# Gated state space: issuing the decay products of a bank's two heads in turn for each key tile

## The chip, the cores and the metric

The kernel runs on one core of a Trainium2 chip. The metric is the time that the device takes for one execution, in microseconds (us). TensorE does the matrix products and writes them to PSUM; VectorE (DVE), ScalarE (ACT) and GpSimd (POOL) work beside it, and the queue of SyncE (SP) issues most of the transfers. Engines wait for each other through semaphores.

## What is computed

The reference is two blocks of two layers each over 512 tokens of width 1024. The change lies in one part of it, the gated state space mixer (Mamba-2) in the second layer of the first block:

```python
xs, Bm, Cm = jnp.split(xbc, [SSM_D_INNER, SSM_D_INNER + G * N], axis=-1)
dt = jax.nn.softplus(dt + dt_bias);  A = -jnp.exp(A_log)
a = (dt * A).reshape(b, nc, CHUNK, G, R)
...
seg = jnp.exp(jnp.where(tril, a_cs[..., :, None] - a_cs[..., None, :], -jnp.inf))
cb = jnp.einsum('bclgn,bcsgn->bcgls', Cm, Bm)
y_diag = jnp.einsum('bcgls,bcgrls,bcsgrp->bclgrp', cb, seg, x_dt)
...
y = y_diag + y_off + xs * D_skip
g = y * jax.nn.silu(z);  g = g * lax.rsqrt(jnp.mean(g * g) + EPS)   # per group
return g @ w_out
```

There are 8 groups of 4 heads, and a head has 64 channels. The kernel computes the same sum without the chunks of 64: for each head one lower triangular matrix over all 512 tokens, decay times C·B, multiplied with x·dt.

## The kernel before

The stage is a loop over 8 groups (group 0, six in a hardware loop of two at a time, group 7). In each group TensorE runs, in this order: `pe_ssm_scores` (turns the two x tiles and makes C·B), `pe_ssm_norm` of the group before, one 256-column unit of the next group's input projection, `pe_ssm_heads(c, 0)`, a second unit, `pe_ssm_heads(c, 1)`, a third unit. A unit is 48 matmuls of 512 columns at lines 529 to 531 (three for each product, with the operands split in a high and a low part). In group 7 the units are the first ones of the output projection.

`pe_ssm_heads(c, m)` works on heads 2m and 2m+1 of the group. Both write one PSUM bank: the even head partitions 0 to 63, the odd head partitions 64 to 127 (`a = (hd % 2) * HD`). For one head there are 4 matmuls, one per key tile i, since a key tile of 128 tokens acts only on the queries from its own start on: 512, 384, 256 and 128 columns. The stationary operand is `XDT`, 128 rows by 64 columns, so that it uses half of the array's columns. `DECAY[:, hd % 2]` is the moving operand. The data is fp32, and the trace shows two passes (a weight load and a matmul each) for one such instruction. So one call is 8 instructions and 16 passes, and there are 16 calls.

What feeds it: VectorE writes the differences of the running sums into `DECAY` (`dve_ssm_decay`, line 2343), ScalarE takes the exponential (line 2305), VectorE multiplies by the masked C·B (`dve_ssm_mask`, line 2351), and counts `masked` up once per head. `DECAY` has two buffers, one for an even and one for an odd head. Before VectorE overwrites the even one for head 2, it waits for `first_head`, which TensorE counts up at the last matmul of head 0. Before it overwrites the odd one for head 3, it waits until the bank of heads 0 and 1 is complete (`bank_ready`). `dve_ssm_output` reads both banks.

The order of VectorE in a group: scores, decay of heads 0 and 1, mask of heads 0 and 1, root of the group before, convolution 0 of the next group (line 2245), decay of 2 and 3, mask of 2 and 3, convolution 1, output. GpSimd splits the weights of the coming units (lines 832 to 837), each as soon as the unit two before it is done, and SP loads the raw weights when GpSimd has split the ones before.

Of the kernel before, what the change touches and what calls it, by code (L numbers as in the profile page):

```python
# [24 lines left out]
NT = SEQ // P  # L25
# [5 lines left out]
HD = 64  # L31
# [202 lines left out]
def build(nc, t, out):  # L234
# [3 lines left out]
    def sem(name):  # L238
        return ctx.enter_context(nc.semaphore(name))
# [252 lines left out]
    bank_ready = sem("bank_ready")  # L492
# [17 lines left out]
    def take_bank(pe, b, turns=0):  # L510

        if b // 4 + (0 if isinstance(turns, int) else 1) > 0:
            pe.e.wait_ge(bank_free[b % 4], turns + b // 4)
        return BANK[b % 4]
# [1690 lines left out]
    def turns(e, n):  # L2205

        return 0 if e is None else e * n
# [49 lines left out]
    def ssm_heads_bank(c, m):  # L2257
        return plan.b["ssm"] + 8 * c + 5 + m
# [20 lines left out]
    def pe_ssm_heads(pe, e, c, m):  # L2279

        w = ssm_sems
        bank = take_bank(pe, ssm_heads_bank(c, m), turns(e, 4))
        for hd in (2 * m, 2 * m + 1):
            a = (hd % 2) * HD
            pe.wait(w["masked"])
            for i in range(NT):
                ins = nc.tensor.matmul(bank[a:a + HD, i * P:SEQ], XDT[:, i, hd * HD:hd * HD + HD],  # L2287
                                       DECAY[:, hd % 2, TRI_AT[i]:TRI_AT[i] + SEQ - i * P], start=i == 0, stop=i == NT - 1)
            if hd == 0:
                ins.then_inc(w["first_head"], 1)  # L2290
            elif hd % 2:
                ins.then_inc(bank_ready, 1)

    def pe_ssm_norm(pe, e, c):
        pe.wait(sq_ready)
# [96 lines left out]
    def pe_ssm(pe):  # L2392
        w = ssm_sems

        def unit(e, c, j):
            if c < SSM_G:
                pe_ssm_unit(pe, e, c, j)
            else:
                pe_ssm_out_unit(pe, 0, j)

        def group(e, c):
            pe_ssm_scores(pe, e, c)
            if c:
                pe_ssm_norm(pe, e, c - 1)
            unit(e, c + 1, 0)
            pe_ssm_heads(pe, e, c, 0)
            unit(e, c + 1, 1)
            pe_ssm_heads(pe, e, c, 1)
            unit(e, c + 1, 2)

        first_unit(pe, plan.u["ssm"], take_pair(pe, plan.p["ssm"]), pe.seen(h_ready))
        pe.passed(h_ready, KD)
        pe_logits(pe, plan.b["dt"], DT_WH, DT_WL, SSM_H, False)
        unit(None, 0, 1)
        pe_dt_rows(pe)
        unit(None, 0, 2)
        pe_dt_columns(pe)
        ssm_program(pe, group, {w["conv_ready"]: 4, w["masked"]: 8, sq_ready: 2})
        pe_ssm_norm(pe, None, SSM_G - 1)
        pe_ssm_out_unit(pe, 0, 3)  # L2420
# [1396 lines left out]
```

## Time and profile before

| | |
|---|---|
| median of 3 runs | 2789.88 us (2789.29 to 2791.4) |
| span of the profiled execution | 2789.68 us |
| TensorE matmul busy | 2515.7 us, 90% of the span |
| VectorE busy | 1800.4 us, 65% |
| GpSimd busy | 1468.6 us, 53% |
| ScalarE busy | 964.0 us, 35% |
| state space stage, from about 680 to 1040 us | 360 us |

The span is the time from the first to the last instruction of one profiled execution. The profile gives no other time for that execution; its span is 0.2 us below the median of the runs. Matmuls are pipelined, and a matmul's record is longer than the distance to the next, so starts are what is to be read, not the sum of durations. "PE" is the matmul and "PEld" the weight load.

### The profile page before, as it was taken

The page shows a single profiled execution, that of the slowest core. Times are in us where ns is not written, and L with a number is a line of the kernel's source. Part 1 is how long each engine was busy: PE and PEld are TensorE (multiplying, and loading weights), DVE is VectorE, ACT ScalarE, POOL GpSimd, SP SyncE. Part 2 cuts the span into 40 slices and gives each one's busy share as a digit, 9 for nine tenths or more (in the row PEclk, how much of TensorE's full clock was granted, in tenths as well). Part 3 has the DMA queues.
Part 4 walks back from the last instruction along what each step waited for, and adds up shares of the span by engine and source line. Part 5 has one row for each costly group of instructions (what it writes and reads, how often), then busy time and mean ns, then how long its engine had stood idle before and what let it go on. Part 6 is the DMA issues. An engine that isn't in the chain of part 4 may idle for free.

```text
span 2789.7 us, 36720 instructions
## 1 busy us (share of the span) xinstructions
PE 2515.7 (90%) x12718; PEld 1994.1 (71%) x12718; DVE 1800.4 (65%) x2200; ACT 964.0 (35%) x1494; POOL 1468.6 (53%) x1234
## 2 busy tenths in 40 slices
PE   4968989968999999899687889999996789999998
PEld 2754767856777778678476558888885678888887
DVE  6669866757676766667678766666136954666324
ACT  2013257733444432577422323222014632222102
POOL 4730333436454443344355216676778937666775
PEclk8977989989999999899888789999998999999999
DMA  8735579952323322699532113333232123333222
GB/s 314 253 128 206 187 252 328 320 177 77 98 83 98 96 77 98 239 335 320 183 80 80 64 53 93 103 90 102 91 109 61 39 54 94 103 91 105 87 94 83
DMA packets 319122, 386.73 MB, mean 139 GB/s; under 512 B 51578, under 2 KB 259214, under 8 KB 318902
## 3 DMA queue, kind: packets, MB, share of 16 engines
q1 hardware_dynamic: 261424, 335.84, 36.8%
q10 hardware_dynamic: 34438, 28.08, 3.3%
q0 software_dynamic: 23168, 21.59, 2.3%
q8 instruction: 57, 0.93, 0.1%
q14 instruction: 35, 0.29, 0.0%
HBM read 397.62 MB, written 55.41 MB: 162 GB/s over the span
## 4 chain that ended last, share of the span: by engine, by line
PE 36%; POOL 19%; issue 17%; DVE 14%; DMA 10%; ACT 2%; SPq 0%; ACTq 0%; POOLq 0%; DVEq 0%
POOL WL L837 14%; PE PAIR L529 6%; PE PAIR L530 5%; PE PAIR L531 5%; POOL WH L833 5%; PE PAIR L1842 4%; DMA RAW<-in_ffn_w_up 3%; PE BANK L529 2%; PE BANK L530 2%; PE BANK L531 2%; PE BANK L2287 2%; DMA RAW<-in_moe_w 2%; PE PAIR L1812 2%; DMA ADA_A<-in_ada_w 2%; DVE ADA_SUM L634 1%
## 5 line engine op out<-in xcount | busy, mean ns | idle before, releaser
L837 POOL TENSOR_TENSOR WL<-RAW,WH 128x512 fp32r<-128x512 f32 x584 | 817.6, 1430 | 12.2
L529 PE MATMUL PAIR<-HH,WH 128*128 128x512 f32 x1792 | 710.6, 397 | 57.2 <-POOL HL L1126 30.8
L530 PE MATMUL PAIR<-HL,WH 128*128 128x512 f32 x1792 | 701.0, 391 | 0.0
L531 PE MATMUL PAIR<-HH,WL 128*128 128x512 f32 x1792 | 700.5, 391 | 0.0
L832 POOL TENSOR_TENSOR TURN<-ONES 128x1 f32<-128x1 f32 x146 | 34.7, 238 | 914.3 <-PE PAIR L531 837.3
L529 PEld LDWEIGHTS PAIR<-HH,WH 128*128 128x128 f32 x1792 | 338.5, 189 | 141.8 <-issue 44.6
L531 PEld LDWEIGHTS PAIR<-HH,WL 128*128 128x128 f32 x1792 | 338.4, 189 | 71.4
L530 PEld LDWEIGHTS PAIR<-HL,WH 128*128 128x128 f32 x1792 | 338.8, 189 | 70.9 <-issue 2.4
L833 POOL TENSOR_SCALAR WH<-RAW 128x2048 fp32r<-128x2048 f32 x146 | 281.0, 1925 | 0.0
L2022 POOL DMA_INDIRECT XG<-htok_scratch,GATHER_I x78 | 106.0, 1359 | 259.0 <-PE PAIR L1812 153.0
L529 PE MATMUL BANK<-WH,GH 128*128 128x256 f32 x624 | 181.0, 290 | 0.0
L530 PE MATMUL BANK<-WL,GH 128*128 128x256 f32 x624 | 173.9, 279 | 0.0
L531 PE MATMUL BANK<-WH,GL 128*128 128x256 f32 x624 | 173.8, 278 | 0.0
L1842 PE MATMUL PAIR<-W2RAW,HT 128*128 128x512 f32 x312 | 147.9, 596 | 6.8 <-ACT HT L1884 5.3
L529 PE MATMUL PAIR<-FHH,WH 128*128 128x512 f32 x352 | 138.7, 394 | 0.0
L531 PE MATMUL PAIR<-FHH,WL 128*128 128x512 f32 x352 | 138.0, 392 | 0.0
L530 PE MATMUL PAIR<-FHL,WH 128*128 128x512 f32 x352 | 136.6, 388 | 0.0
L1949 DVE TENSOR_TENSOR WL<-RAW,WH 128x1024 fp32r<-128x1024 f32 x78 | 95.6, 1226 | 57.1 <-ACT WH L1760 57.1
L1943 DVE TENSOR_TENSOR GL<-PAIR,GH 128x1024 fp32r<-128x1024 f32 x78 | 95.5, 1224 | 52.5 <-ACT GH L1878 52.5
L1812 PEld LDWEIGHTS PAIR<-IDENT,XG 128*128 128x128 f32 x624 | 83.3, 192 | 60.9 <-issue 34.4
L2832 DVE TENSOR_TENSOR X<-PAIR,X 128x1024 f32<-128x1024 f32 x8 | 9.8, 1225 | 179.3 <-PE PAIR L531 179.3
L2794 DVE TENSOR_TENSOR PAIR<-PAIR,RSTD 128x1024 f32<-128x1024 f32 x44 | 54.2, 1232 | 110.0 <-PE PAIR L531 109.9
(530 smaller groups left out, 4878.2 us busy)
## 6 DMA issues: line engine op xcount, KB each, us to landing
RAW<-in_moe_w SPq DMA_DIRECT2D x156, 512.0 KB, 6.9
RAW<-in_ffn_w_up SPq DMA_DIRECT2D x88, 512.0 KB
W2RAW<-in_moe_w SPq DMA_DIRECT2D x78, 512.0 KB, 6.1
ADA_B<-in_ada_w SPq DMA_DIRECT2D x30, 1024.0 KB, 5.4
RAW<-in_ssm_w_in SPq DMA_DIRECT2D x48, 512.0 KB
ADA_A<-in_ada_w SPq DMA_DIRECT2D x18, 1024.0 KB, 7.3
RAW<-in_ffn_w_down SPq DMA_DIRECT2D x32, 512.0 KB
RAW<-in_ev_w_in SPq DMA_DIRECT2D x20, 512.0 KB
```

What stands on the lines that cost most here:

```text
L529: nc.tensor.matmul(o, wh, xh, start=start, stop=False)
L530: nc.tensor.matmul(o, wh, xl, start=False, stop=False)
L531: return nc.tensor.matmul(o, wl, xh, start=False, stop=stop)
L833: pool.tensor_scalar(WH[:, s], RAW[:, s], 1.0, 1.0, ALU.mult, ALU.mult).then_inc(split_hi, 1)
L837: ins = pool.tensor_tensor(WL[:, s, c], RAW[:, s, c], WH[:, s, c].bitcast(F32), ALU.subtract)
L1812: ins = nc.tensor.transpose(pair[:, k // 4, (k % 4) * P:(k % 4) * P + P], rows_of(s)[:, :, k], IDENT[:])
L1842: ins = nc.tensor.matmul(pair[:, m, :], HT[:, s % 2, :], W2RAW[:, s % 2, c], start=True, stop=True)
L1943: dve.e.tensor_tensor(GL[:, s % 2].rearrange("p (b k) n -> p b (k n)", b=2), PAIR[p % 2][:], GH[:, s % 2].rearrange("p (b k) n -> p b (k n ...
L1949: dve.e.tensor_tensor(WL[:, u % 2, 0:D], RAW[:, u % 2, 0:D], WH[:, u % 2, 0:D].bitcast(F32), ALU.subtract).then_inc(w["w1_low"], 1)
L2022: pool.e.indirect_dma_start(XG[:, s % 2, :], None, htok_dram, bass.IndirectOffsetOnAxis(ap=GATHER_I[:, s:s + 1], axis=0), bounds_check=SEQ ...
L2287: ins = nc.tensor.matmul(bank[a:a + HD, i * P:SEQ], XDT[:, i, hd * HD:hd * HD + HD], DECAY[:, hd % 2, TRI_AT[i]:TRI_AT[i] + SEQ - i * P], ...
L2794: dve.e.tensor_tensor(pair[:], pair[:], bcast(RSTD[:], 1, 2), ALU.mult).then_inc(w["scaled"], 1)
```

## The change

The two heads of a bank were issued one after the other, each behind its own wait for `masked`. Now one wait for both stands ahead, and for each key tile the even head's matmul is followed by the odd head's. The operands, the places in PSUM, the number of matmuls and their start and stop flags stay. `first_head` is counted up at head 0's last matmul as before, which is now the last but one of the call; `bank_ready` at the last matmul of the call.

```diff
-        for hd in (2 * m, 2 * m + 1):
-            a = (hd % 2) * HD
-            pe.wait(w["masked"])
-            for i in range(NT):
+        pe.wait(w["masked"], 2)
+
+        for i in range(NT):
+            for hd in (2 * m, 2 * m + 1):
+                a = (hd % 2) * HD
                 ins = nc.tensor.matmul(bank[a:a + HD, i * P:SEQ], XDT[:, i, hd * HD:hd * HD + HD],
                                        DECAY[:, hd % 2, TRI_AT[i]:TRI_AT[i] + SEQ - i * P], start=i == 0, stop=i == NT - 1)
-            if hd == 0:
-                ins.then_inc(w["first_head"], 1)
-            elif hd % 2:
-                ins.then_inc(bank_ready, 1)
+                if hd == 0 and i == NT - 1:
+                    ins.then_inc(w["first_head"], 1)
+        ins.then_inc(bank_ready, 1)
```

## Rows read from the trace of the kernel before

**Rows 1.** Busy time by stretch; columns: PE, PEld, DVE, ACT, POOL, clock, DMA

```profile
680.00:1040.00 360.00, 359.30 (x1545) 263.32 (x1544) 266.10 (x354) 146.07 (x141) 171.46 (x142) 1.00 0.30 92
1040.00:1110.00 70.00, 70.00 (x322) 56.34 (x320) 39.49 (x67) 20.94 (x32) 31.22 (x30) 0.98 0.24 83
```

**Rows 2.** Who waited for whom, 680 to 1040 us: total, times, longest

```profile
POOL TURN L832 <- PE PAIR L531: 182.0, 23, 9.1
ACT CONV L2224 <- PE PAIR L531: 53.2, 14, 4.4
...
DVE XDT L2321 <- PE BANK L2269: 45.1, 7, 7.2
...
PE PAIR L529 <- DVE HL L2525: 0.7, 1, 0.7
```

**Rows 3.** Groups of instructions by shape, TensorE, 680 to 1040 us

```profile
L2287 PE MATMUL BANK<-DECAY,XDT 128*64 128x512 f32 x64 | 34.3, 618 | 0.0
```

**Rows 4.** Chain of work that ended last, 737.1 to 741.2 us: start, us, what

```profile
737.25 2.30 PE BANK L2287 x8
739.55 0.10 issue
739.65 1.46 PE BANK L2287 x6
741.11 0.43 PE PAIR L529
```

**Rows 5.** The same chain, 680 to 1040 us: turns, then C·B

```profile
767.18 0.87 PE BANK L2269 x8
768.05 2.16 PE BANK L2275 x8
```

**Rows 6.** Timeline of the weight loads of one bank, from 751.2 us

```profile
752.14 0.19 PEld L2287 LDWEIGHTS BANK<-DECAY,XDT 128*64 128x64 f32 x2 [0.35 <-issue]
752.63 0.14 PEld L2287 LDWEIGHTS BANK<-DECAY,XDT 128*64 128x64 f32 x1 [0.29 <-issue]
...
753.70 0.62 PEld L2287 LDWEIGHTS BANK<-DECAY,XDT 128*64 128x64 f32 x6 [0.18 <-issue]
754.62 0.14 PEld L2287 LDWEIGHTS BANK<-DECAY,XDT 128*64 128x64 f32 x1 [0.29 <-issue]
```

**Rows 7.** Timeline of TensorE: 32-column tiles in turn, and full-width turns

```profile
2146.37 2.02 PE L3313 MATMUL BANK<-HF,IDENT 128*32 128x128 f32 x32 [1.11 <-DVE HF L1149]
...
767.02 1.03 PE L2269 MATMUL BANK<-IDENT,CONV 128*128 128x128 f32 x8
```

**Rows 8.** Timeline around the second bank of a group: TensorE, then VectorE

```profile
752.14 3.93 PE L2287 MATMUL BANK<-DECAY,XDT 128*64 128x512 f32 x16
756.00 0.50 PE L529 MATMUL PAIR<-HH,WH 128*128 128x512 f32 x1
...
733.98 3.34 DVE L2372 RECIPROCAL RSTD<-RSTD 128x512 f32<-128x512 f32 x1
...
743.61 3.13 DVE L2343 TENSOR_SCALAR DECAY<-ACS_ROW,ACS_COL 128x512 f32<-128x512 f32 x8
747.41 2.89 DVE L2351 TENSOR_TENSOR DECAY<-DECAY,CBM 128x1280 f32<-128x1280 f32 x2 [0.67 <-ACT DECAY L2305]
```

**Rows 9.** Timeline of group 7 and of a first bank: TensorE, then VectorE

```profile
1012.11 3.93 PE L2287 MATMUL BANK<-DECAY,XDT 128*64 128x512 f32 x16
...
1009.58 2.88 DVE L2351 TENSOR_TENSOR DECAY<-DECAY,CBM 128x1280 f32<-128x1280 f32 x2
...
816.38 5.41 DVE L2343 TENSOR_SCALAR DECAY<-ACS_ROW,ACS_COL 128x512 f32<-128x512 f32 x8
```

**Rows 10.** Chain of work, 998 to 1005 us: TensorE released by VectorE

```profile
998.74 1.56 DVE HL L2525
1000.30 0.14 issue
```

**Rows 11.** Waits of SP's queue, 1040 us to the end

```profile
SPq L683 <- POOL WL L837: 1027.2, 98, 42.3
```

## Prediction

> **What bounds the kernel now.** I read the busy time by stretch first. From 680 to 1040 us, which holds the whole state space stage, TensorE is busy 359.3 of 360 us at a granted clock of 1.00 of full speed, that is at the upper level of 2.4 GHz; VectorE has 266 us, ScalarE 146, GpSimd 171 [rows 1]. Then the waits of that stretch: the long ones all belong to other engines that wait for TensorE (GpSimd 182.0 us, ScalarE 53.2, VectorE 45.1), while TensorE's one wait of note is 0.7 us, for the split input of group 7 [rows 2]. So the stage ends when TensorE's instructions are through, and time taken out of TensorE's stream comes out of the span one to one, until another engine is late.
>
> Next, how long a bank of decay products takes. Its matmuls are 128 rows by 64 columns of stationary operand; the records of the widest last 618 ns each, though their starts are closer together [rows 3], so I go by starts and by the chain. The timeline has one at 752.14 and the next unit's first matmul at 756.00: 3.86 us [rows 8]. All 16 banks have this length (the same record of 3.93 us stands at 752.14 and at 1012.11 [rows 8, 9]). Their 16 passes are not simply added up: the chain shows head 0's eight passes as 2.30 us, then 0.10 us of issue, then only six passes in 1.46 us, and the next unit [rows 4]. Head 1 also has eight passes, so its first two, the widest, lie beside head 0's. The weight loads show where: in the bank at 752.14, two loads come together, then one by one, each as its matmul starts; at 753.70 six stand back to back, and then single ones again at 754.62 [rows 6]. A load row lists passes in order of time, so the six are head 0's last three and head 1's first three. **At the crossing from head 0 to head 1 the array works on both heads at once**, one in the lower and one in the upper half of its columns. If they ran one after the other, the bank would take 2.30 us plus the cost of the same columns without an overlap: C·B has eight passes of the same widths (512, 384, 256, 128, two each) and takes 2.16 us in the chain [rows 5], so 2.30 + 2.16 = 4.46 us. The bank of today already saves 0.60 us against that, by the one crossing.
>
> Why only one crossing: head 1's first pass gets in when head 0's fifth starts and the load of its sixth is issued, the first of the six. So only what stands behind a few pending instructions of head 0 gets in. In the order of today the second head's instructions lie behind all four of the first head's; in the new order each is next to its partner.
>
> **The change part by part.**
>
> The order. With the heads in turn both halves of the array have work from the start to the end of the bank. Head 0's eight passes last as long as alone (2.30 us by the chain), and head 1's run beside them. What goes is the issue gap and head 1's tail: 0.10 + 1.46 = 1.56 us [rows 4]. Head 1 begins a moment after head 0; I take 0.02 us for this, an estimate, since loads issued back to back in the six-load row leave room for little more (0.62 us for six loads of about 0.14 us each, which overlap in part) [rows 6]. Gain of a bank: 1.54 us. 16 banks: 24.6 us.
>
> Do two halves keep full speed when both are busy throughout? The trace has the nearest case in another stage: at 2146.37 four tiles of 32 columns are issued in turn, 32 passes of 128 columns, in 2.02 us; eight full-width passes of 128 columns, one after the other, take 1.03 us [rows 7] and 0.87 us net in the chain [rows 5], 0.109 us each. One after the other the 32 would take 24 x 0.109 + 1.03 = 3.65 us. So issuing in turn does let the tiles run together, and four of them give 3.65 / 2.02 = 1.8 times the speed, or about two tiles' worth. Two tiles should then reach nearly two. Bounds: the best end is 1.56 us a bank (25.0 in all). The other end takes that ratio of 2.02 / 3.65 = 0.55 as it stands, with all its start and end in it, though 32 short passes suffer more from these than a bank does: 4.46 x 0.55 = 2.47 us instead of 2.30, a gain of 3.86 - 2.47 = 1.39 us, 22.2 us in all. I take the value near the best end, as the crossing of rows 4 is the same instruction, tile and data type, and there head 0's passes keep their length.
>
> The wait. `masked` for both heads now stands ahead of head 0. Nothing is queued behind it on TensorE that could go ahead of it; the unit before it is already issued. It costs nothing where both masks are there when TensorE arrives. First banks: the bank at 737.25 [rows 4] has VectorE begin the reciprocal that stands behind both its masks at 733.98 [rows 8], some 3 us early, and nothing before that bank becomes faster within the group. Second banks: the masks end at 747.41 + 2.89 = 750.30 and TensorE arrives at 752.14, 1.84 us later [rows 8]. Now TensorE arrives 1.54 us sooner, as counted from the end of the unit that starts this chain (ScalarE's read, VectorE's convolution, decay, exponential, mask). 0.30 us is left, and a hand-over from VectorE to TensorE takes up to 0.14 us where the chain shows one [rows 10]. So the cover just holds: 0. It is thin; each 0.1 us by which the chain slips behind costs 0.7 us over the seven second banks that have this layout. Group 7, first bank: TensorE arrives at 1012.11 and the second mask ends at 1009.58 + 2.88 = 1012.46 [rows 9]. Head 0 could start with the first mask alone; now it waits 0.35 us and the hand-over: 0.4 us lost, once. That group's second bank has masks of VectorE's own pace and more room after this delay; I take 0.
>
> The signals. `first_head` comes with head 0's last pass, as before some 2.3 us after the bank's start; it is now also slightly behind head 1's sixth. `bank_ready` comes 1.54 us sooner. VectorE meets neither late: head 2's decay starts at 743.61, more than 4 us after both [rows 8]. Nothing else moves: no DMA, no instruction of another engine and no queue is passed; TensorE issues one wait less.
>
> What is late next: GpSimd and the transfers follow TensorE. GpSimd waited 182 us in 23 places for a unit, about 8 us each [rows 2], and will wait up to 1.5 us less. After the stage TensorE is busy 70.0 of 70 us [rows 1], and later SP's loads wait for GpSimd's splits, 98 times [rows 11], so that all that follows moves forward as one piece. I keep the whole gain.
>
> **The sum**: 24.6 - 0.4 = 24.2 us. The profiled span is 2789.7 us and the median of the runs 2789.9, so both lose the same, and the forecast is 2789.9 - 24.2 = 2765.7 us.
>
> **The rivals.**
>
> Partly together. Two halves share something that slows each, and the gain of a bank is below 1.39 us. For it: four tiles reach only 1.8 times. Against it: this is what a limit of two streams would give, and two halves are two streams. Its time: 22.2 - 0.4 gives 2768.1 at the bound above; with half of the gain, 12.3 - 0.4, 2778.0. The Trainium skill, "TensorE: Matmul & The Clock Gate", section "Measured speedup vs the span model", has three column tiles at 2.38 times, 0.79 of the ideal; by that (an estimate) two would give 1.59 times, and the sum would come to about 2773.
>
> The thin cover fails. The eight decay instructions take 3.13 us ahead of a second bank [rows 8], but 5.41 us at another place, where GpSimd works beside them [rows 9]. Were they 2.3 us longer at seven second banks, TensorE would wait 2.3 - 0.16 = 2.1 us in each, 15 us: 2780.7. Against it: GpSimd's split and this chain both start from the same unit's end, so they lie to each other as before.
>
> Slower: the halves don't overlap when issued in turn, and the one overlap of today is lost too. It would be so if a load for the other half had to wait for the matmul that runs, and the crossing were a case of its own, say because head 0 had nothing more to load. Then each bank takes 4.46 us, 0.60 more; 16 x 0.60 + 0.4 = 10.0 us, 2799.9. It decides as soon as a bank takes over 3.86 us. Against it stands the row with four tiles in turn, which is 1.8 times faster than one after the other [rows 7]. The Trainium skill, same page, section "The mechanism", states that weight loads overlap matmuls in flight only where the row group differs, and that matmuls start and end strictly in order; both heads use all 128 rows, so by that rule this rival would hold. The trace disagrees with it: the six loads at 753.70 run while head 0's passes do [rows 6].
>
> No change: the order in the stream is not what decides and every bank keeps its 3.86 us: 2790.
>
> **How the numbers follow.** The full overlap 0.80; partly together 0.09 (two thirds of it up to 2773); thin cover 0.04; no change 0.02; slower 0.05. The range reaches from 2762, a little below the best end of the bounds (2789.9 - 25.0 = 2764.9), since a shift of all later stages may move their transfers by some us either way, to 2773, which takes in the partial case's larger part. About 0.2% (5.6 us) is what a measurement of this kernel can tell from no change. Faster by more than this: 0.80 + 0.09 + 0.04 = 0.93; within it 0.02; slower 0.05.
>
> **What the profile after would show.** A bank's record at the changed line lasts about 2.4 us from its first start to the next unit's first matmul at about 2.32 instead of 3.86. Its weight loads come in pairs of heads. The chain has no issue gap within a bank. VectorE's masks end some 0.3 us before the second banks; in group 7 TensorE waits about 0.4 us for the mask. The stage as a whole is some 24 us shorter. A bank of 2.5 to 3.1 us means partly together; 4.4 slower; a wait for line 2351 in most groups means the cover was too thin. If all banks are short and the span is not, a later stage took the gain back.

## The result, and the profile after

The changed kernel takes 2766.69 us (median of 4 runs, 2762.97 to 2770.92) against 2790.64 us before (4 runs in the same comparison): a ratio of 0.9914, with a 95% interval of 0.9902 to 0.9926. That is 24.0 us less (20.7 to 27.3 by the interval), where 24.2 us and 2765.7 us were forecast.

The profiled execution has a span of 2764.1 us. Its matmuls at line 2288 are those of line 2287 before. Here is the timeline of TensorE and then of its weight loads at the second bank of group 1, which answers to [rows 6] and [rows 8]:

```profile
745.78 2.37 PE L2288 MATMUL BANK<-DECAY,XDT 128*64 128x512 f32 x16
748.09 0.50 PE L529 MATMUL PAIR<-HH,WH 128*128 128x512 f32 x1
...
745.78 0.20 PEld L2288 LDWEIGHTS BANK<-DECAY,XDT 128*64 128x64 f32 x4 [0.35 <-DVE DECAY L2351]
746.26 0.14 PEld L2288 LDWEIGHTS BANK<-DECAY,XDT 128*64 128x64 f32 x2 [0.29 <-issue]
746.69 0.14 PEld L2288 LDWEIGHTS BANK<-DECAY,XDT 128*64 128x64 f32 x2 [0.29 <-issue]
747.01 0.14 PEld L2288 LDWEIGHTS BANK<-DECAY,XDT 128*64 128x64 f32 x2 [0.18 <-issue]
747.34 0.57 PEld L2288 LDWEIGHTS BANK<-DECAY,XDT 128*64 128x64 f32 x6 [0.18 <-issue]
748.08 0.19 PEld L529 LDWEIGHTS PAIR<-HH,WH 128*128 128x128 f32 x1 [0.17 <-issue]
```

From the bank's first start to the next unit's is now 748.09 - 745.78 = 2.31 us (2.304 in the records), where it was 3.86. The loads come in pairs: two take the time of one (0.14 us), since one is for the lower and one for the upper half of the array. The chain of work, which answers to [rows 4], has all 16 passes in one piece and no issue gap:

```profile
745.62 0.23 PE PAIR L531
745.85 2.30 PE BANK L2288 x16
748.15 0.43 PE PAIR L529
```

2.30 us is what the chain gave head 0's eight passes before [rows 4]. In the records of both kernels these eight start at the same distances from the start of the bank (0, 0.48, 0.91, 1.23, 1.55, 1.77, 1.99 and 2.10 us); each pass of head 1 now starts 7 ns behind its partner of head 0. So head 1 costs next to nothing. All 16 banks have this length.

Where the time went is read from three stretches of the profiled executions, in us: up to the first bank, from there to the first unit behind the last bank, and from there to the end.

| | up to the first bank | the banks' stretch | behind it |
|---|---|---|---|
| before | 691.6 | 339.3 | 1758.8 |
| after | 689.9 | 315.0 | 1759.1 |

24.3 us are gone from the middle one, and the stretch behind it keeps its length: nothing is given back. The 1.7 us in the first stretch don't come from the change, since the code up to there is the same. In the ten profiled executions of this case, of ten kernels that are alike there, this stretch took 689.5 to 694.9 us, and the one behind the banks 1757.0 to 1764.2.

### The profile page after: what moved, and what is told of

Same layout as the page of the kernel before. It is cut to its first block, busy times and chain, and to the rows that moved or that the text cites. A ratio compares the mean times of both kernels' runs of the same rounds, so it can differ in the third digit from the quotient of the medians.

```text
span 2764.1 us, 36708 instructions
## 1 busy us (share of the span) xinstructions
PE 2495.0 (90%) x12718; PEld 1986.0 (72%) x12718; DVE 1801.5 (65%) x2200; ACT 964.4 (35%) x1494; POOL 1469.9 (53%) x1234
## 4 chain that ended last, share of the span: by engine, by line
PE 35%; POOL 20%; issue 18%; DVE 14%; DMA 9%; ACT 2%; SPq 0%; ACTq 0%; POOLq 0%; DVEq 0%
POOL WL L837 14%; PE PAIR L529 6%; PE PAIR L530 5%; PE PAIR L531 5%; POOL WH L833 5%; PE PAIR L1842 4%; PE BANK L529 2%; PE BANK L530 2%; PE BANK L531 2%; DMA RAW<-in_ffn_w_up 2%; DMA RAW<-in_moe_w 2%; PE PAIR L1812 2%; DVE ADA_SUM L634 1%; PE BANK L2288 1%; DVE ADA_SUM L632 1%
## 5 line engine op out<-in xcount | busy, mean ns | idle before, releaser
L1812 PEld LDWEIGHTS PAIR<-IDENT,XG 128*128 128x128 f32 x624 | 83.4, 192 | 59.4 <-issue 34.3
```

What stands on the lines that cost most here:

```text
L1812: ins = nc.tensor.transpose(pair[:, k // 4, (k % 4) * P:(k % 4) * P + P], rows_of(s)[:, :, k], IDENT[:])
```

## The experiments

### One wait ahead of the bank, heads one after the other (wait_only)

```diff
-        for hd in (2 * m, 2 * m + 1):
+        pe.wait(w["masked"], 2)
+        for hd in (2 * m, 2 * m + 1):
             a = (hd % 2) * HD
-            pe.wait(w["masked"])
             for i in range(NT):
```

> The kernel before with one wait for both masks ahead of the bank and head 0 still whole before head 1. Theory (overlap of the array's halves makes the gain, the wait only costs): each bank keeps 3.86 us, nothing is gained, and only group 7's first bank starts later, by about 0.5 us (mask at 1012.45 us, plus a hand-over of 0.146 us as group 7 of the changed kernel shows, against a start at 1012.11). Time 2791.1 against 2790.6 us, no difference that can be measured. Rival (the second wait in the middle of a bank held head 1 back): banks become shorter than 3.86 us, towards 2.3, and the time falls by up to 24 us.

Measured: 2791.31 us against 2791.59, ratio 0.9999 (0.9989 to 1.0009), no difference. The chain of a bank is the one of before, to 0.01 us:

```profile
753.04 2.30 PE BANK L2287 x8
755.34 0.10 issue
755.44 1.46 PE BANK L2287 x6
```

The stretch of the banks is 339.8 us, 0.5 us longer, all of it ahead of group 7's first bank, which waits for the second mask:

```profile
1013.44 3.90 PE L2287 MATMUL BANK<-DECAY,XDT 128*64 128x512 f32 x16 [0.42 <-DVE DECAY L2351]
```

So the wait has no part in the gain, and its price is the 0.5 us that theory gave.

### In turn, but both heads in the lower half of the array (same_half)

```diff
-                a = (hd % 2) * HD
+                a = 0
...
-                                       ..., start=i == 0, stop=i == NT - 1)
+                                       ..., start=i == 0 and hd % 2 == 0, stop=i == NT - 1 and hd % 2 == 1)
```

> The changed kernel, heads in turn for each key tile, but both heads write partitions 0 to 63, so both use the same half of the array's columns; the odd head's result is added to the even head's and the upper 64 channels are left out. Theory (it is the two halves of the array, not the order of issue): 16 passes one after the other, a bank takes about 4.43 us (2.30 of eight passes plus 2.13 for 2560 more columns at the same pace), the time is 16 x 2.13 = 34 us above the changed kernel's 2766.7, so 2800 to 2801 us. Rival (the order alone, or the data's order in memory, makes it fast): a bank stays at 2.30 us and the time at 2767.

Measured: 2802.37 us, ratio to before 1.0036 (1.0025 to 1.0047), so slower than before. A bank is one piece of 4.45 us in the chain:

```profile
757.30 4.45 PE BANK L2288 x16
761.75 0.43 PE PAIR L529
```

The order of issue, the operands in memory and the number of instructions are those of the changed kernel. What differs is where the odd head's result goes: the other columns of the array and, tied to them, the other partitions of the bank. The run doesn't tell these two apart. That both heads add to the same places is no price of its own: the eight passes more cost 2.15 us, and C·B's eight of the same widths, which go to places of their own, took 2.16 [rows 5]. The bank goes from 2.30 to 4.45 us, and the banks' stretch from 315.0 to 349.3 us, 34.3 us more. So the overlap of the two halves is the whole of the gain. This is also the price of the slower rival measured: 4.46 us was worked out for a bank without any overlap.

### How far head 1 may lie behind (two_tiles, three_tiles)

The loop runs over another order of (head of the bank, key tile). The first line with a plus is that of two_tiles, the second that of three_tiles:

```diff
-        for i in range(NT):
-            for hd in (2 * m, 2 * m + 1):
+        for odd, i in ((0, 0), (0, 1), (1, 0), (1, 1), (0, 2), (0, 3), (1, 2), (1, 3)):   # two_tiles
+        for odd, i in ((0, 0), (0, 1), (0, 2), (1, 0), (0, 3), (1, 1), (1, 2), (1, 3)):   # three_tiles
+            for hd in (2 * m + odd,):
```

> The changed kernel with another order in a bank: two key tiles of head 0, two of head 1, again two and two. Theory (one matmul in work and one waiting for each half): head 0's first two fit, head 1's follow at once, both halves are fed throughout; bank 2.30 to 2.35 us, time as the changed kernel, 2767 us. Rival (only the strict alternation lets the halves overlap): a bank between 2.6 and 3.9 us.

> The changed kernel with another order in a bank: head 0's key tiles 0, 1, 2, then head 1's 0, head 0's 3, head 1's 1, 2, 3. Theory (instructions are handed on in order, and each half of the array takes one fp32 matmul in work and one waiting): head 0's third must wait until its second starts, 0.91 us into the bank (0.48 + 0.43), and head 1 starts right behind it; a bank takes 0.91 + 2.30 = 3.21 us, 16 x 0.91 = 14.5 us over the changed kernel, some 2781 us. Rival (a window of many instructions that can start out of order, limited only by their number): head 1 starts at once, since it is now one instruction nearer than in the kernel before or in the middle between, at a time that fits no start of head 0's second; bank 2.3 to 2.8 us.

Measured: with two tiles of head 0 ahead a bank takes 2.355 us and the run 2766.65 us; with three ahead 3.213 us and 2778.28 us (one run each; for the second 2781 was expected, and single runs of one kernel lie up to 10 us apart). The banks' stretches are 315.8 and 329.9 us, so three_tiles adds 14.9 us to the changed kernel's, with 14.5 expected. The weight loads of three_tiles show where head 1 gets in:

```profile
748.17 0.19 PEld L2288 LDWEIGHTS BANK<-DECAY,XDT 128*64 128x64 f32 x2 [0.35 <-issue]
748.65 0.14 PEld L2288 LDWEIGHTS BANK<-DECAY,XDT 128*64 128x64 f32 x1 [0.29 <-issue]
749.08 0.46 PEld L2288 LDWEIGHTS BANK<-DECAY,XDT 128*64 128x64 f32 x4 [0.29 <-issue]
```

At 749.08 head 0's third pass starts, which is the first of its second matmul, and at that moment four loads come together: head 1's begin 0.91 us into the bank (749.08 - 748.17), and 0.91 + 2.30 = 3.21. One rule gives all four orders: instructions are handed on in their order, and a half of the array takes one fp32 matmul in work and one waiting. A third one of the same half blocks everything behind it until the second starts. (The first column counts head 0's matmuls, of two passes each.)

| head 0's matmuls ahead of head 1's first | head 1 starts when | bank by the rule | measured |
|---|---|---|---|
| 1 (the change) | at once | 2.30 | 2.304 |
| 2 | at once | 2.30 | 2.355 |
| 3 | head 0's second starts, 0.91 | 3.21 | 3.213 |
| 4 (before) | head 0's third starts, 1.55 | 3.85 | 3.858 |

The 0.05 us over at two tiles fit the rule too. Here head 0's fourth matmul is the one that must wait, until its third starts at 1.554 us, and head 1's third stands behind it. So that one's first load isn't done ahead, as in the changed kernel; in this bank, which starts at 745.86, there is one load at 747.10 where the changed kernel has a pair, and the missing one is in the row of seven:

```profile
747.10 0.14 PEld L2288 LDWEIGHTS BANK<-DECAY,XDT 128*64 128x64 f32 x1 [0.17 <-issue]
747.42 0.63 PEld L2288 LDWEIGHTS BANK<-DECAY,XDT 128*64 128x64 f32 x7 [0.18 <-issue]
```

By the records that load starts at 1.559 us in the bank and the next one at 1.614 (1.562 in the changed kernel), and the pass that needs the latter starts at 1.828 instead of 1.777 us, which is the 0.05. That the rule is the chip's own mechanism is not shown; four orders of one bank agree with it. Nor do they tell one matmul waiting from two passes waiting.

### Half of the odd head's work left out (half_odd)

```diff
         for i in range(NT):
-            for hd in (2 * m, 2 * m + 1):
+            for hd in ((2 * m, 2 * m + 1) if i in (0, NT - 1) else (2 * m,)):
```

> The changed kernel without the odd head's key tiles 1 and 2 (their products are left out); the order else is kept. Theory (the odd head's work lies wholly beside the even head's): the bank keeps its 2.30 us with 1280 of the odd head's 2560 pass columns gone, and the time stays at 2766 us. Rival (the halves share something and slow each other in part): the bank gets shorter, by up to 0.2 us, and the time by up to 3 us.

Measured: a bank takes 2.297 us, 7 ns less than with the whole odd head, for four passes fewer; the run 2768.42 us (one run) and the banks' stretch 314.8 against 315.0 us. The partner is free to 7 ns, which is the distance by which head 1's passes start behind head 0's in the changed kernel's records. Head 0's eight passes start at the same distances here as there, though four of them have no partner now. So the halves don't slow each other.

```profile
749.15 2.30 PE BANK L2288 x11
751.45 0.43 PE PAIR L529
```

### How thin the cover of the mask is (late_mask_before, late_mask_after)

In either kernel:

```diff
             conv(e, c + 1, 0)
+            if not last:
+                dve.e.tensor_tensor(TMP[:], TMP[:], TMP[:], ALU.max)
             dve_ssm_decay(dve, e, c, (2, 3))
```

> The kernel before with an idle VectorE instruction of 1024 columns, 1.25 us, ahead of the decay of heads 2 and 3 in groups 0 to 6. Theory (cover of 1.84 us ahead of the second banks, of which a hand-over takes 0.15): nothing waits, time as before, 2790.6 us. Rival (VectorE's own load is felt somewhere else in the stage): each of 7 groups longer by up to 1.25 us, 2799.

> The changed kernel with the same idle VectorE instruction of 1.25 us ahead of the decay of heads 2 and 3 in groups 0 to 6. Theory (the changed kernel has 0.28 us from mask to start, of which the hand-over is 0.15, so 0.14 is left): seven second banks (group 0's has 0.7 us more cover than the six others) start 1.1 us late each, about 6 x 1.1 + 0.4 = 7.0 us in all, 2773.7 us. Rival (the cover is not thin, since VectorE's chain moves with TensorE): no wait, 2767.

Measured: on the kernel before 2792.12 us, ratio 1.0001 (0.9991 to 1.001), nothing; its banks' stretch is 339.3 us, unchanged. On the changed kernel 2774.03 us (4 runs, 2770.60 to 2778.23), 0.9931 of before (0.9915 to 0.9948). TensorE now waits at the second banks:

```profile
748.79 1.50 DVE DECAY L2351
750.28 0.04 issue
750.33 2.37 PE BANK L2288 x16
752.70 0.43 PE PAIR L529
```

The direction is as expected; the size is not. The stretch of the banks grew by 318.5 - 315.0 = 3.5 us where 7.0 were expected. The runs can't decide: the median lies 7.3 us above the changed kernel's, but each against the kernel before in its own comparison (18.4 us less here, 24.0 us less there) gives 5.6 us, and either interval is several us wide. The profiled execution, the slowest of the four, was also longer by 3.7 us ahead of the first bank and by 5 us behind the last, where nothing was changed. I go by the stretch. The timeline of VectorE in late_mask_after shows why 3.5:

```profile
742.86 1.99 DVE L2470 TENSOR_TENSOR TMP<-TMP 128x1024 f32<-128x1024 f32 x1
744.77 2.45 DVE L2343 TENSOR_SCALAR DECAY<-ACS_ROW,ACS_COL 128x512 f32<-128x512 f32 x8
747.38 2.89 DVE L2351 TENSOR_TENSOR DECAY<-DECAY,CBM 128x1280 f32<-128x1280 f32 x2 [0.16 <-ACT DECAY L2305]
```

The added instruction took 1.99 us, not 1.25, but the decay instructions take 2.45 us instead of the 3.13 of before [rows 8]. By the records these are the same 0.7 us: in the kernels without the addition the first of the eight decay instructions, which runs as GpSimd's last split ends, takes 1.16 to 1.23 us in the hardware loop and its like 0.47; with the addition it is the added instruction that runs at that moment, and the first decay instruction takes 0.47. And the mask, which had waited 0.67 us for ScalarE anyway [rows 8], now waits 0.16. So the masks came only 0.7 us later. In the changed kernel the start of a second bank lies 0.31 us behind the end of the mask in five of the six groups of the hardware loop, and 0.28 in the first; with the late mask it is 0.056 in all six. So 0.25 us of cover was left, and about 0.5 us was paid in each of six groups and 0.36 in group 0: 3.3 us.

### The variance of the group before put behind the masks in group 7 (mask_first)

```diff
-            if c:
+            if c and not last:
                 dve_ssm_variance(dve, e, c - 1)
             dve_ssm_mask(dve, (0, 1))
+            if last:
+                dve_ssm_variance(dve, e, c - 1)
```

> The changed kernel with VectorE's instruction for the variance of group 6 (0.68 us) put behind the masks of heads 0 and 1 in group 7, where TensorE waits for the second mask. Theory (group 7's first bank starts 0.49 us late for it): that bank starts 0.49 us sooner relative to the one before, 30.58 instead of 31.06 us after it; in the time, 0.5 us, nothing that can be measured. Rival (the bank waits for something else): it starts at the same place.

Measured: group 7's first bank starts 30.73 us behind the bank before it, with 31.06 in the changed kernel, so 0.33 us of the 0.49 come back; 2767.56 us in one run, no difference that can be measured. The mask is still what TensorE waits for, since it now waits for ScalarE:

```profile
988.00 2.89 DVE L2351 TENSOR_TENSOR DECAY<-DECAY,CBM 128x1280 f32<-128x1280 f32 x2 [0.17 <-ACT DECAY L2305]
```

## Why the prediction was right

**The bound.** TensorE filled the stage, and every us out of its stream came out of the stage. Right: the shorter banks take 24.3 us out of the stretch, and in same_half the longer ones put 34.3 us in; 16 times the change of a bank is 24.9 and 34.4 us.

**The overlap.** Read from one crossing in each bank [rows 4, 6] and the four tiles in another stage [rows 7]. Right: a bank was forecast at 2.32 us and is 2.304. Head 1 lies 7 ns behind head 0, where 20 ns were allowed; the reading behind the 20 was loose, since the six loads of that row aren't back to back (by the records they start at 1.556, 1.559, 1.614, 1.772, 1.988 and 2.042 us in the bank). 16 x (3.858 - 2.304) = 24.9 us, 24.6 forecast. The lower bound taken from the row of four tiles (2.47 us) was too cautious: half_odd shows that two halves don't slow each other, and 4.451 / 2.304 = 1.93 times the speed is more than the rival "partly together" allowed.

**The wait.** Second banks: no wait was forecast, and 0.30 us of room. Right: they start 0.31 us behind the mask, with the units before them as long as in the kernel before. The loader's row above is marked as released by VectorE, but its 0.35 us are the same 0.35 us that stand before the change as "issue" [rows 6]: the name of a releaser is no proof of a wait, the distance to the work before is. Group 7: 0.4 us forecast, 0.49 measured.

```profile
986.26 2.81 DVE DECAY L2351 x2
989.08 0.14 issue
989.21 2.37 PE BANK L2288 x16
```

The term that was short is the hand-over, which was taken as half seen: 0.34 us of missing mask [rows 9] and 0.15 us to the start.

**What was wrong in the thin cover.** The rule "each 0.1 us by which the chain slips costs 0.7 us over seven banks" holds for a slip of the mask itself. It was then carried over to a longer instruction of VectorE, as if all of that arrived at the mask. The chain had 0.67 us of its own in it, ScalarE's exponential, and late_mask_after cost half of what was expected, by the stretch. Nor are the seven second banks alike: in group 0 the changed kernel starts the second bank 0.98 us behind its mask, not 0.31. The prediction gave 0.16 us of cover, 0.30 less a hand-over of 0.14; it is 0.25, since the hand-over inside the hardware loop took 0.056.

**The rest moves as one piece.** Right: 1758.8 us behind the last bank before, 1759.1 after.

**How close the number is.** The terms were each right within 0.3 us: 24.9 us gained by the banks, where 24.6 were forecast, and 0.49 us lost in group 7, where 0.4 were; the two differences have opposite signs. That the medians then agree with the forecast to about 1 us in the time and 0.2 us in the gain is luck in part, as the interval of the gain is nearly 7 us wide.

The slower rival rested on a real price (4.45 us measured, 4.46 worked out) and failed on its condition. The Trainium skill, "TensorE: Matmul & The Clock Gate", section "The mechanism", has weight loads overlap matmuls only where the row group differs, and matmuls strictly in order. In this kernel both heads use all 128 rows, and the loads of one half run beside the matmuls of the other. That alone doesn't refute the section, as the prediction took it to: it also allows a load into a background weight buffer, and in same_half, where all is in one half, loads run beside matmuls as well (the third pass's load starts at 0.482 us in the bank, the second pass at 0.480). What the runs contradict is the strict order: in half_odd the instruction issued last starts, and by its record ends, ahead of one issued before it (last section).

## What to carry to other kernels

Where two fp32 products with 64 stationary columns each go to different halves of PSUM's partitions, issue them in turn, with at most two matmuls of one half ahead of the other's. Here they then ran side by side at full speed, and a bank took 2.30 us, where it had 3.86 with one crossing and 4.45 with no overlap. A start that comes too early in the trace for its place in the program (six passes in the chain where eight were issued) was here the sign that such an overlap exists and is cut short by the order. Before a wait is moved ahead, count the room at each place where it stands, and follow a slip through the waits of the chain before pricing it.

## What the runs showed of the hardware

Matmuls for different halves need not start in program order. In the kernel before, head 1's first two passes start at 1.56 and 2.04 us in the bank and head 0's last at 2.10. In half_odd they don't end in it either, by the records, whose ends the profile works out: the odd head's last instruction, the last of the bank, has its two passes at 750.64 and 750.80 us by the records, while the even head's last two start at 751.07 and 751.18. The row of loads at 750.64 holds that instruction's two:

```profile
750.64 0.57 PEld L2288 LDWEIGHTS BANK<-DECAY,XDT 128*64 128x64 f32 x5 [0.18 <-issue]
751.38 0.19 PEld L529 LDWEIGHTS PAIR<-HH,WH 128*128 128x128 f32 x1 [0.17 <-issue]
```

The instruction that counts `bank_ready` up was through at about 751.07 by its record, but the semaphore's event stands at 751.48, just behind the end of the even head's last pass (751.45). It is so in all 16 banks of that run: the event comes 0.41 to 0.43 us behind the end of its own instruction's record and 0.03 to 0.06 us behind the end of the even head's. In the kernel before, where head 1's last pass ends 1.56 us behind head 0's, the event comes 0.014 us behind its own record's end. So the signal came in program order though the work did not. That it does so in other orders and kernels was not tried.

The hand-over from VectorE to TensorE had two sizes: 0.056 us in the six groups of the hardware loop (late_mask_after), 0.147 us in groups 0 and 7 outside it, in all kernels where TensorE waited there. What makes the difference is open.
